# Moving small modulation sums and half products to other places in an fp32 two-block transformer kernel

## What is computed

```python
# block 1 (depth 1)
sh1, sc1, g1, sh2, sc2, g2 = split(silu(c) @ w_ada + b_ada, 6)      # modulation, 6 x 2048
h = modulate(rms_norm(x, norm_mix_pre), sh1, sc1)
p = h @ w_in                             # r, k, v, decay/a/gate loras, MLA inputs, gates
y_rwkv = rwkv_branch(...)                # bidirectional RWKV-7, 16 heads of 64
o      = mla attention(...)
x = x + g1 * rms_norm((g_rwkv * (y_rwkv @ w_rwkv_proj) + g_mla * (o @ w_mla_proj)) @ w_out)
x = x + g2 * rms_norm(conv_ffn(modulate(rms_norm(x), sh2, sc2)))
# block 2 (depth 2), each layer:
shift, scale, gate = split(silu(cond) @ w_ada_2 + b_ada_2, 3)       # for x and for the context
p = (rms_norm(x) * (1 + scale) + shift) @ w_in_2
x = x + gate * (concat(pooling branch, differential attention branch) @ w_out_2)
```

## Time and profile before

| | us |
|---|---|
| median of 3 runs | 3972.62 |
| lowest, highest | 3971.62, 3973.78 |
| profiled execution, its own time | 3977.09 |
| its span | 3975.4 |
| TensorE busy | 3721.8 (94%) |
| VectorE busy | 2688.7 (68%) |
| ScalarE busy | 1724.4 (43%) |
| mean granted TensorE clock | 0.975 |

### The profile page before, as it was taken

One profiled execution on the slowest core, in us unless ns is written; L12 is line 12 of the kernel. 1 busy time (PEld: TensorE's weight loads), 2 busy tenths in 40 slices (PEclk: granted clock), 3 DMA queues, 4 the chain that ended last, 5 costly groups with the idle time before them and its releaser, 6 DMA issues.

```text
span 3975.4 us, 84227 instructions
## 1 busy us (share of the span) xinstructions
PE 3721.8 (94%) x34998; PEld 3199.8 (80%) x34998; DVE 2688.7 (68%) x4743; ACT 1724.4 (43%) x3140; POOL 252.0 (6%) x441
## 2 busy tenths in 40 slices
PE   6999999788888999989999999899999999899999
PEld 2788778666666999989999999887777778777879
DVE  2544477766666786888888888767666643767375
ACT  2544323534344454455444444542433442524354
POOL 0000021111111000000000000000000000010000
PEclk7999999899999999999999999999999999999999
DMA  9422588231322786756777677545235133573336
GB/s 372 151 80 62 206 284 262 78 99 56 100 63 82 240 270 218 240 168 212 233 221 241 217 233 230 193 154 181 74 127 163 60 131 96 162 231 117 117 101 191
DMA packets 290011, 667.54 MB, mean 168 GB/s; under 512 B 21152, under 2 KB 31392, under 8 KB 287600
## 3 DMA queue, kind: packets, MB, share of 16 engines
q1 hardware_dynamic: 233392, 441.73, 34.6%
q0 software_dynamic: 56256, 220.58, 17.6%
HBM read 644.40 MB, written 17.83 MB: 167 GB/s over the span
## 4 chain that ended last, share of the span: by engine, by line
PE 73%; DVE 10%; DMA 9%; issue 4%; ACT 3%; SPq 0%; POOL 0%; POOLq 0%; DVEq 0%; ACTq 0%
PE psum L891 57%; DMA red_own<-in_w_adaT 2%; DVE wlo L2238 2%; PE psum L1153 2%; DMA red_a<-in_w_adaT 2%; DMA ada_head<-in_w_ada 1%; PE psum L1203 1%; DMA ada_raw<-in_w_ada 1%; PE psum L857 1%; PE psum L916 1%; ACT whi L1593 1%; DVE junk_l L2254 1%; DMA red_raw<-in_w_adaT 1%; PE psum L1084 1%; DVE smx L3038 1%
## 5 line engine op out<-in xcount | busy, mean ns | idle before, releaser
L1593 ACT ACTIVATE whi<-raw 128x512 fp32r<-128x512 f32 (+3 forms) x1568 | 970.7, 623 | 1469.3 <-PE psum L891 1425.9
L2238 DVE TENSOR_TENSOR wlo<-raw,whi 128x512 fp32r<-128x512 f32 (+3 forms) x1568 | 1042.2, 680 | 737.3 <-ACT whi L1593 726.5
L891 PE MATMUL psum<-hhi,whi 128*128 128x512 f32 (+1 forms) x2416 | 835.9, 346 | 55.9 <-DVE wlo L2238 27.2
L891 PE MATMUL psum<-hlo,whi 128*128 128x512 f32 (+1 forms) x2416 | 814.3, 337 | 0.0
L891 PE MATMUL psum<-hhi,wlo 128*128 128x512 f32 (+1 forms) x2416 | 814.1, 337 | 0.0
L891 PEld LDWEIGHTS psum<-hhi,whi 128*128 128x128 f32 x2416 | 462.9, 192 | 158.5 <-DVE wlo L2238 58.0
L891 PEld LDWEIGHTS psum<-hhi,wlo 128*128 128x128 f32 x2416 | 462.9, 192 | 48.1
L891 PEld LDWEIGHTS psum<-hlo,whi 128*128 128x128 f32 x2416 | 463.5, 192 | 46.5 <-issue 2.2
L891 PE MATMUL psum<-fhi,whi 128*128 128x256 f32 x1408 | 402.6, 286 | 12.9 <-DVE wlo L2238 8.3
L891 PE MATMUL psum<-flo,whi 128*128 128x256 f32 x1408 | 400.7, 285 | 0.0
L891 PE MATMUL psum<-fhi,wlo 128*128 128x256 f32 x1408 | 400.7, 285 | 0.0
(11 more groups left out here) (459 smaller groups left out, 6950.2 us busy)
## 6 DMA issues: line engine op xcount, KB each, us to landing
raw<-in_w_in SPq DMA_DIRECT2D x328, 512.0 KB, 4.3
red_raw<-in_w_adaT POOLq DMA_DIRECT2D x115, 512.0 KB, 5.2
raw<-in_w_out SPq DMA_DIRECT2D x96, 512.0 KB, 3.8
raw<-in_w_gate SPq DMA_DIRECT2D x88, 512.0 KB, 5.1
raw<-in_w_val SPq DMA_DIRECT2D x88, 512.0 KB, 4.3
raw<-in_w_down SPq DMA_DIRECT2D x88, 512.0 KB, 5.3
ada_head<-in_w_ada SPq DMA_DIRECT2D x64, 512.0 KB, 10.3
red_own<-in_w_adaT POOLq DMA_DIRECT2D x64, 512.0 KB, 6.2
```

Source lines behind the costliest of these rows:

```text
L891: mm = pe.matmul(dst, l, r, start=(k == 0 and i == 0 and first), stop=(k == nch - 1 and i == 2), skip_group_check=True)
L1593: act.activation(whi[:, lc % HL, 0:width], raw[:, (lc // 2) % RAW, lc % 2, 0:width], ACT.Copy).then_inc(w_hi, 1)
L2238: dve.tensor_tensor(wlo[:, lc % HL, 0:width], raw[:, (lc // 2) % RAW, lc % 2, 0:width], whi[:, lc % HL, 0:width].bitcast(F32), ALU.subtrac ...
```

## The change

- `RED_KV` 16 to 15, `RED_LORA` 10 to 13, a new `RED_RPROJ` (1 sum in each section of rproj), `RED_MPROJ` 4 to 5, `RED_A` (10, 20, 10) to (12, 22, 10). The FFN has 121 sums and not 133.
- The last 32 sums leave layer 1's first heads (`qkva1`) and lie in layer 0's output product (`out0`), 0, 11, 11 and 10 in its four sections. They use `red_raw`. `cond_c` is loaded when `mix` has been split.
- GpSimd asks for a section's loads of sums before it waits for its stores, and for `cond_keep` after that. Around `x1` the loads are grouped otherwise.
- `ada_raw` has three buffers. Half products 0 and 1 lie before `level_b(1, 1)`, 2 before the turn of `k_s`, 3 before `last_y_b`; 4 to 7 stay in the tail.

```diff
-ADA_RAW = 2
+ADA_RAW = 3
-RED_KV, RED_R, RED_LORA, RED_GATE, RED_MPROJ, RED_WOUT = 16, 3, 10, 7, 4, 8
+RED_KV, RED_R, RED_LORA, RED_GATE, RED_RPROJ, RED_MPROJ, RED_WOUT = 15, 3, 13, 7, 1, 5, 8
-RED_VALUES, RED_A, RED_B, RED_C = 8, (10, 20, 10), (21, 21, 0), (2, 20, 10)
+RED_VALUES, RED_A, RED_B, RED_C = 8, (12, 22, 10), (21, 21, 0), (0, 11, 11, 10)
...
@@ pool, key to lora sections, after the four stores @@
+                reduce_own(n_red, base + n)
+                n_red = max(n_red, base + n)
                 for m in range(4):
                     pool.wait_ge(sh_st[m], p_ * 16 + 16)
@@ pool, pair @@
+                for kh in range(ADA_RAW, 2 * ADA_RAW):
+                    ada_half("w_ada", col, it, 0, kh)
                 pool.wait_ge(rw_dve, at(RW_DVE, "bv", it, len(FIRST_DVE)))
@@ pool, around x1 @@
-            reduce_in(RED_EARLY + 4 + 2 * RED_GATE, RED_EARLY + 7 * RED_GATE + 4)
+            reduce_in(RED_EARLY + 4 + 2 * RED_GATE, RED_EARLY + 7 * RED_GATE + 3)
             pool.wait_ge(o_in, 16)
+            reduce_in(RED_EARLY + 7 * RED_GATE + 3, RED_EARLY + 7 * RED_GATE + 6)
             pool.wait_ge(s_lo, 4 + 8)
             pool.dma_start(x1[:, :, :], A["xT"][:, :, TOK:T2]).then_inc(x1_in, 16)
@@ pool, block 2 @@
                 if l == 0:
                     pool.dma_start(xall[:, :, :], x2_keep).then_inc(x2_in, 16)
                     pool.wait_ge(x2_in, 16)
+                    pool.wait_ge(s_lo, 24)
+                    pool.dma_start(cond_c[:, :], cond_keep[:, 0, :]).then_inc(cond_in3, 16)
+                    reduce_in(RED_BOTH, RED_ALL)
+                    pool.wait_ge(cond_in3, 48)
@@ vector, rproj @@
+                    if j:
+                        reduced(lo_reduced.n, both_of(cond_l), [junk_1[:, :]])
+                        lo_reduced.n += 1
@@ vector, mproj @@
-                    if i % 2:
+                    if i % 2 or i == 8:
@@ vector, heads @@
-                    late_n = (RED_A, RED_B)[it] if l == 0 else (RED_C, (0, 0, 0))[it]
+                    late_n = (RED_A, RED_B)[it] if l == 0 else (0, 0, 0)
@@ vector, out_add @@
                         lo(c, (LA + i,))
+                        for _ in range((i + 1) * RED_C[it] // 16 - i * RED_C[it] // 16 if l == 0 else 0):
+                            reduced(lo_reduced.n, [cond_c[:, :]], [junk_1[:, :]])
+                            lo_reduced.n += 1
```

More of the change, by code:

```diff
@@ L231, in build @@
         wlo = sb("wlo", [P, HL, N], 24, F32R)
-        ada_raw = [sb(f"ada_raw{i}", [P, 2, N], kb) for i, kb in enumerate((32, 36))]
+        ada_raw = [sb(f"ada_raw{i}", [P, 2, N], kb) for i, kb in enumerate((32, 36, 60.5))]
         red_raw = [sb(f"red_raw{i}", [P, HALF], 32 + 4 * i) for i in range(2)]
@@ L703, in ada_half @@
                 if not isinstance(it, int) or it > 0 or c >= ADA_RAW:
-                    pool.wait_ge(ada_used, 8 * ADA_PAIR * it + c - ADA_RAW + 1 + 8 * ADA_HEAD)
+                    before = c - ADA_RAW if c >= ADA_RAW else next(k for k in range(7, 0, -1) if k % ADA_RAW == c) - 8
+                    pool.wait_ge(ada_used, 8 * it + before + 1 + 8 * ADA_HEAD)
                 if not isinstance(it, int):
@@ L779, in pair @@
                     values_in(v1)
-                for kh in range(ADA_RAW, 8):
+                for kh in range(2 * ADA_RAW, 8):
                     ada_half("w_ada", col, it, 0, kh)
@@ L834, in _ @@
                     pool.wait_ge(cond_in3, 32)
[L835 to L838, removed]
                 pool.wait_ge(at_dve[l], 2 * len(AT_DVE[l]))
@@ L1259, in _ @@
                 turn(a_s[0], "ta0")
+                ada(0, 0, 1)
                 level_b(1, 1)
@@ L1272, in _ @@
                 level_xy(0, 2)
+                ada(0, 2)
                 dve_at("ce")
@@ L1304, in _ @@
                 key_norms_out(done, act_at)
+                ada(0, 3)
                 last_y_b()
@@ L2141, in heads @@
                             hi(c, range(48, 48 + LA))
-                        if it == 0 and i == 2:
-                            act.wait_ge(red_done, (RED_TURN, RED_ALL)[l])
+                        if l == 0 and it == 0 and i == 2:
+                            act.wait_ge(red_done, RED_TURN)
                         for m in range(4):
@@ L2957, in late @@
                             reduced(lo_reduced.n, both_of(cond_a), [junk_1[:, :]], red_a)
-                        elif lo_reduced.n < RED_BOTH:
+                        else:
                             reduced(lo_reduced.n, [cond_b[:, :], cond_a[:, 1, :]], [junk_1[:, :]], red_b)
-                        else:
-                            reduced(lo_reduced.n, [cond_c[:, :]], [junk_1[:, :]], red_a)
                         lo_reduced.n += 1
@@ L2977, in ropes @@
                             done(TT(qk[:, b, TOK:T2], rope2[:, 0, :], rope2[:, 1, :], ALU.add), f"t{b}", it)
-                    if l != it:
-                        dve.wait_ge(cond_in3, 32 + 16 * l)
+                    if l == 0 and it:
+                        dve.wait_ge(cond_in3, 32)
                     for i in range(16):
@@ L3084, in _ @@
                 dve.wait_ge(sg_done, 16 * l + 16)
-                if l:
-                    dve.wait_ge(red_done, RED_ALL)
                 def out_add(it, ahead):
                     c = C0[f"out{l}"] + it * 16
+                    if l == 0 and it == 1:
+                        dve.wait_ge(cond_in3, 48)
                     for i in range(13 + ahead):
```

20 lines of the change are left out of this document (8 added, 12 removed).

## The result

The changed kernel takes 3920.95 us (median of 4 runs, 3915.31 to 3926.81), the kernel before, timed beside it, 3972.19. The ratio is 0.9871, 95% interval 0.9853 to 0.9888: 51 us less, where 37.5 were forecast. The profiled execution took 3926.81 us, span 3925.1.

What follows compares the result with a forecast made beforehand. TensorE's own work fills three quarters of the span; only its idle or low-clock time can change. Terms -15 + 5 - 11 + 0.5 - 16 + 1 - 2 = -37.5 us take 3972.6 to 3935; range 3922 to 3957.

Steps and rivals of the forecast that it cites:

- Part 1: Layer 1's first heads: moving 32 sums out ends TensorE's 13.2 us of waits; -15 us (-13 to -17).
- Part 2: Layer 0's output product: the 32 sums cost time only at three section ends; +5 us (0 to +12).
- Part 3: Key, value and r stages: earlier sum loads, 15 sums a section, -11 us (-15.4 to -4); lora +0.5.
- part 5: mproj: x1 asked for earlier, +1 us (-1 to +4); FFN: twelve sums fewer, -2 us (0 to -4).
- Part 4: Pair loop: half products fill TensorE's waits in the levels and leave the tail; -16 us (-22 to 0).
- 2 of the 3.6: Layer 1's first heads: of 3.6 us of full clock lost, 2 us counted as gained.
- 1.14 + 0.84 = 2.0 us a pair: Pair's tail: halves 0 and 1 gone save 1.14 us, second chunk step comes 0.84 us earlier.
- they cost nothing as long as the clock is high: Pair's levels: halves 0 to 3 need 1.14, 0.57 and 0.57 us, under waits of 1.4, 0.8 and 1.2 us.
- rival D: Emptier state loop: TensorE stays at 1.2 GHz, some 6 us more a pair; 3983 us; chance 0.04.
- A: Pair's tail: late copies behind the solves leave part 4 at 0; 3951 us; chance 0.13.
- B: Output product's loads late (+12), key stage bound by its load rhythm (-4); 3949 us; chance 0.14.
- C: Pair loop: sixth and seventh half products wait for their load, part 4 is -6; 3945 us; chance 0.05.

Runs made afterwards that it cites:

- out_spread: late_loads with the output product's sums only after the first 14 of 16 chunks of a section: 3903.58 us, ratio 0.9827.
- late_loads: Changed kernel, but GpSimd loads halves 3, 4 and 5 only after VectorE's last mask of level 3: 3908.02 us, ratio 0.9840.
- x1_early: Kernel before, but x1 asked for when oT's last part is split, ahead of the loads of mproj's first sums: 3972.36 us, ratio 1.0002.
- no_pair: Changed kernel with part 4 undone (two buffers, all eight halves in the tail): 3923.78 us, ratio 0.9879.
- again: The changed kernel once more, unedited, timed beside the kernel before: 3917.58 us, ratio 0.9865.
- pair_only: Kernel before with part 4 alone (three buffers, half products 0 to 3 in the levels): 3959.75 us, ratio 0.9973.

## Why the prediction missed, point by point

The mechanisms of parts 1 to 3 were right. The step that failed most is in part 5: the FFN's term took a share of its waits by the number of sums, -2, and the stage gave -11. Part 4 failed the other way, by loads that its own early half products start.

- **Part 1, forecast -15, measured -20.** The waits were counted right (13). Of the low clock the step took "2 of the 3.6" us, in one stretch of 45 us. Over the whole layer it was worth 5 (4 to 5 over all traces). Some 2 us more are in neither count.
- **Part 2, forecast +5, measured +4.** Right, with its mechanism: out_spread takes it away.
- **Part 3, forecast -11, measured -12 to -14.** Right. Half of it belongs to the sixteenth sum, which the text named only in passing.
- **Part 4, forecast -16, measured -7 in the traces and -6 to -11 in the times.** The step "1.14 + 0.84 = 2.0 us a pair" for the tail was short of the 2.5 measured. The step that failed is "they cost nothing as long as the clock is high", for the halves in the levels. They did lie under the waits for `yinv` and `fin`: with the loads moved (late_loads) the last level product comes at 38.63 us, before at 38.54. But their early use started loads while TensorE's next instructions were due, and it then stood 1.3 to 1.6 us more a pair. I had written only that the loads come a pair ahead, and had not asked when the next ones go out. The clock was the smaller loss, in the tail, and the forecast gave it to rival D alone.
- **Part 5, forecast +1 for `x1`, measured -5 in mproj.** The bound said -1. Two things failed. I let the load behind `x1` be late, and did not see that the change's grouping puts three sums' loads ahead of it. And I took ScalarE's waits for weights (5.8 us) to move with `x1`; they fell to 3.0, and the stage lost 3 us even with the load late (x1_early). In the whole kernel's time x1_early shows nothing, within 4 us.
- **Part 5, forecast -2 for the FFN, measured -11.** This is the largest miss. I took a share of the 8.3 us of waits for twelve sums in 133. The waits are not shared out over the sums: most of their time sat at the third sum of a group, and the twelve sums were nearly all of these. TensorE's waits for `wlo` went from 8.3 to 2.4 us. The clock is not the rest: the stage had 16 us at 1.2 GHz before and 12.5 after, but three other traces with 133 sums had 12.0 to 12.8 and still took 782.9 to 784.9 us (before 784.8 by the same count, after 773.6). Some 3 us more lie in steps between products that took over 0.13 us at the full clock and are not listed as waits, 49 before and 26 after. What is left, under 3 us, stays open.
- **Rivals.** A, B and C did not come about as written; C's -6 for part 4 is near what no_pair gives, but without the waits for loads that C meant. D's direction is in the traces (12.5 us a pair at 1.2 GHz against 7.5, less in again and pair_only), at about 1 us a pair and not 6.
- **The range** ended at 3922, and its own bounds do not give that: "all low bounds but one" is 53 to 57 us less than 3972.6, 3916 to 3920. With that sum the measured 3921 lies inside, and by luck: three terms passed their bounds (part 1, `x1`, the FFN), each bounded by the waits or a little more, and part 4 stayed short. The parts add up: -11, -17, -4 and -15 from the four runs of single parts, and some 6 for the counts in the key stage, make -53; measured -51 and -54.

## What to carry to other kernels

Before saying that work placed in a gap is free, look at what its end releases: a buffer that comes free earlier starts a transfer earlier, and the question is what is moving or being fetched then. Do not share out waits for loads over the work: find the place in the rhythm where buffers run out, and ask whether the change removes that place, not what share of the work it removes. Look at the clock behind the waits stage by stage: in layer 1 it was worth 4 to 5 us beside 13 us of waits, in the FFN nothing that other traces bear out.

## What was not expected of the hardware

- TensorE stopped for 0.5 to 2.7 us with no releaser in runs of 64x64 products (14166 matmuls in 552 us), at distances of 127 to 129 matmuls or a multiple. These stops in a pair's first 20 us were 0.50 us with no weight load there and 1.8 to 2.0 us with 1 MB moving. They ended 1.3 to 1.55 us after a packet of 16 KB on the instruction queue, which started 1.3 us later when the 1 MB was moving.
- The same kernel's pair loop took 552.2 and 542.9 us in two executions, with some 12 and 10 us a pair at 1.2 GHz. A difference of 5 us in one profile of this stage says nothing by itself.
- Two half products of 0.57 us in a loop of 9 us moved the time at 1.2 GHz from 8.7 to 10.3 us a pair (three traces) to 6.8 (one).
